# Storing each expert's result with one GpSimd transfer of both halves instead of two

## The reference, cut to what matters

```python
combine = jnp.sum(jax.nn.one_hot(eidx, N_EXPERTS, dtype=jnp.float32) * wk[..., None], axis=1)
y = jnp.zeros((n, dm), jnp.float32)
for e in range(N_EXPERTS):
    h = jax.nn.silu(xn @ w_gate[e]) * (xn @ w_up[e])
    y = y + combine[:, e:e + 1] * (h @ w_down[e]).astype(jnp.float32)
return x + y.reshape(b, l, dm).astype(x.dtype)
```

## Time and profile before

| | |
|---|---|
| median of 3 runs | 1045.94 us (1045.46 to 1047.20) |
| the profiled execution: its time | 1046.94 us |
| its span, first to last instruction | 1045.1 us |
| PE busy | 807.7 us (77%) |
| DVE, ACT, POOL busy | 251.0, 117.8, 148.8 us |
| moved by DMA over the span | 277.47 MB, mean 265 GB/s |
| stores of L493 | 64 of 128 KB |

### The profile page before, as it was taken

One profiled execution on the slowest core, in us unless ns is written; L12 is line 12 of the kernel. 1 busy time (PEld: TensorE's weight loads), 2 busy tenths in 40 slices (PEclk: granted clock), 3 DMA queues, 4 the chain that ended last, 5 costly groups with the idle time before them and its releaser, 6 DMA issues. The chain is left out here.

```text
span 1045.1 us, 9777 instructions
## 1 busy us (share of the span) xinstructions
PE 807.7 (77%) x3738; PEld 469.3 (45%) x3739; DVE 251.0 (24%) x699; ACT 117.8 (11%) x200; POOL 148.8 (14%) x283
## 2 busy tenths in 40 slices
PE   3899999922999899870898787888787787877810
PEld 2688888812988644370333233333233332333300
DVE  4729325754111112224010000000000000000036
ACT  4010121000200011200110010100010100001012
POOL 6300009800023300003010000000000000000040
PEclk9899999965999999955898999999998989889965
DMA  9994114200240170264499999999999999999661
GB/s 345 401 312 162 44 48 128 81 0 1 107 161 1 40 302 1 97 245 174 198 389 428 428 425 430 428 427 428 425 429 428 428 426 428 428 427 426 268 208 68
DMA packets 47643, 277.47 MB, mean 265 GB/s; under 512 B 12186, under 2 KB 13030, under 8 KB 35315
## 3 DMA queue, kind: packets, MB, share of 16 engines
q1 hardware_dynamic: 35388, 238.67, 55.8%
q0 software_dynamic: 11568, 36.58, 9.2%
q10 hardware_dynamic: 646, 1.64, 0.4%
HBM read 243.62 MB, written 33.26 MB: 265 GB/s over the span
## 5 line engine op out<-in xcount | busy, mean ns | idle before, releaser
L1333 PE MATMUL ps<-arena 128*64 128x512 f32 x1024 | 257.9, 661 | 85.7 <-DMA arena<-in_w_exp_up 84.6
L1141 PE MATMUL ps<-arena 128*128 128x272 f32 x1024 | 242.3, 398 | 0.0
L1141 PEld LDWEIGHTS ps<-arena 128*128 128x128 f32 x1024 | 197.2, 193 | 41.2
L1333 PEld LDWEIGHTS ps<-arena 128*64 128x64 f32 x1024 | 89.8, 152 | 231.6 <-issue 229.8
L1071 DVE COPY arena<-ps 128x512 f32<-128x512 f32 x32 | 22.1, 692 | 434.4 <-PE ps L1346 434.4
L1346 PE MATMUL ps<-arena 128*64 128x512 f32 x512 | 116.5, 595 | 1.1 <-DVE arena L1067 1.1
L493 POOL DMA_DIRECT2D y_rows<-arena x64 | 33.2, 523 | 472.4 <-DVE arena L1071 471.5
L1282 PE MATMUL ps<-arena 128*128 128x512 f32 (+1 forms) x160 | 71.1, 605 | 2.9 <-POOL arena L481 2.9
L1346 PEld LDWEIGHTS ps<-arena 128*64 128x64 f32 x512 | 38.1, 137 | 64.2 <-issue 61.2
L699 DVE TENSOR_TENSOR arena<-arena 128x256 f32<-128x256 f32 (+11 forms) x173 | 56.9, 329 | 25.0 <-DMA arena<-in_ssm_b_im 19.2
L651 ACT ACTIVATE arena<-ps 128x512 f32<-128x512 f32 x32 | 19.1, 597 | 330.1 <-PE ps L1333 330.1
(11 more groups left out here) (177 smaller groups left out, 505.1 us busy)
## 6 DMA issues: line engine op xcount, KB each, us to landing
arena<-in_w_exp_gate SPq DMA_DIRECT2D x32, 2048.0 KB, 29.0
arena<-in_w_exp_up SPq DMA_DIRECT2D x32, 2048.0 KB, 19.5
arena<-in_w_exp_down SPq DMA_DIRECT2D x32, 2048.0 KB, 24.6
x_rows<-arena POOLq DMA_DIRECT2D x25, 512.0 KB, 14.3
arena<-in_w_in SPq DMA_DIRECT2D x6, 2048.0 KB, 13.4
arena<-x_rows SPq DMA_DIRECT2D x16, 512.0 KB, 19.4
y_rows<-arena POOLq DMA_DIRECT2D x64, 128.0 KB, 7.1
y_rows<-arena POOLq DMA_DIRECT2D x9, 512.0 KB, 27.2
```

Source lines behind the costliest of these rows:

```text
L1141: last = pe.matmul(dst[:, hh, 0:HALF], w[:, k, m * P:(m + 1) * P], rhs[:, k, hh * HALF:(hh + 1) * HALF], start=(k == 0), stop=(k == kk - 1))
L1333: last = pe.matmul(ps[n * TILE:(n + 1) * TILE, 2 + par, :], x_t[:, k, :], w[:, k, :], start=(k == 0), stop=(k == KD - 1))
```

## The change

L493: the two stores of 64 rows x 512 columns become one of 128 x 512. On the HBM side the 64 x 1024 block is viewed with the half as the outermost dimension (2 x 64 x 512), so that it matches the partitions of `y_sb` in order. The counts waited for are halved with it, at L496 and at L1078. The stores of the overflow path (L503) are left as they were.

```diff
             for e in range(NE):
                 pool.wait_ge(y_ready, e + 1)
-                for half in range(2):
-                    pool.dma_start(y_rows[e * TILE:(e + 1) * TILE, half * F:(half + 1) * F],
-                                   y_sb[e % 2][half * TILE:(half + 1) * TILE]).then_inc(y_stored[e % 2], 16)
+                pool.dma_start(y_rows[e * TILE:(e + 1) * TILE, :].rearrange("t (h n) -> h t n", h=2),
+                               y_sb[e % 2]).then_inc(y_stored[e % 2], 16)
             for par in range(2):
-                pool.wait_ge(y_stored[par], 32 * NP)
+                pool.wait_ge(y_stored[par], 16 * NP)
...
                 if e >= 2:
-                    dve.wait_ge(y_stored[e % 2], 32 * (e // 2))
+                    dve.wait_ge(y_stored[e % 2], 16 * (e // 2))
```

## The result

The changed kernel took 1064.64 us (median of 4, 1061.70 to 1070.19) against 1046.02 (median of 4) for the kernel before on the same chip: a ratio of 1.0178, 95% interval 1.0140 to 1.0215, +18.6 us. The forecast was 1051.5 us, range 1045 to 1060. The direction was right, the size was short by 13 us. The profiled execution took 1061.70 us, with a span of 1059.9.

The account below looks back on a forecast made before the run. The expert loop was taken as bound by the weight stream. 0 (steps 1 to 3) + 1.8 (late weights) + 0 (y_sb wait) + 3.8 (end) = +5.6 us, from the median of 1045.94 to 1051.5 us; range 1045.0 to 1060.0.

Parts of the forecast that it names:

- What bounds the loop: Expert loop: a weight stream at 425 to 430 GB/s; POOL or DVE time costs nothing, later weights are paid in full.
- Step 1: POOL's store issue: one 0.52 us instruction fewer per expert, 31 hidden, the last -0.5 us; bytes and packet number unchanged.
- Step 2: Merged store: outermost dimension 2 puts the whole 128 x 512 store on two DMA engines, 32 packets each.
- step 4: Weights behind the store in the loop: equal engine totals over 8 experts, lateness +1.8 us at the last wait, between 0 and 4.3.
- Step 3: Which two engines on POOL's queue: successive stores move on around the 16, two further each time.
- fixed pair: Rival: the same two engines carry every store, 20.2 us work per expert against 15.9, 1170 us; chance 0.09 including overlapping pairs.
- store chain: Rival: stores landing after over 31.2 us make the L1078 wait the bound, 1075 us or over 1250; chance 0.10.
- Step 5: DVE's wait on y_sb (L1078): a store lands in 26 to 30 us, on average 31.2 allowed; cost 0.
- Step 6: The end, last store to gathers: 32 packets on two engines without weights, +3.8 us including the -0.5 for issue.

Follow-up runs that it names:

- run on ACT's queue: The changed kernel with its single store led by 2 issued by ACT on its own queue (q10) instead of POOL: 1176.70 us, 1.1271.
- 16-engine run: The changed kernel with the HBM side viewed as 128 contiguous pieces, so both sides are led by 128; a probe of time only: 1044.32 us, 0.9985.
- filler run: The kernel before plus, per expert but the last, one tiny GpSimd transfer led by 2 (128 pieces of 16 bytes) into unused scratch: 1059.31 us, 1.0114.
- last-store run: The kernel before, with only the last expert's store made the single transfer led by 2: 1051.62 us, 1.0056.

## Why the prediction was wrong

**What bounds the loop** was right: it is the weight stream, and DVE's new waits are cover. **Step 1** (POOL's issue) was mis-sized and of no weight: the single instruction takes 0.80 us, not 0.52, and 0.23 us of the end's gap were saved instead of 0.5.

**Step 2**, two engines, was right, and read from rows of another queue: 53 GB/s during the last store, and 49 to 52 GB/s in the run on ACT's queue where only two engines had work left. What the Trainium skill states ("DMA: Bandwidth & Descriptors", on why a DMA increments its semaphore by 16) agrees: the largest number up to 16 that divides both leading dimensions. The Trainium skill's rule for kernel authors on the same page, to use one transfer over 128 partitions in place of two over halves, holds in the 16-engine run (1044.32 us) and fails in the changed kernel, which has 128 partitions on one side only.

The step that failed in the main is the last sentence of **step 1**, "The bytes and the packets' number stay the same", taken into **step 4** as "every engine gets the same total over 8 experts". Only the data was counted. GpSimd's queue put packets on the 14 engines without data too (448 per store), by their sizes 64 descriptors on each, as many as the two with data have, and at about 6 ns these cost the weight stream 0.4 us per expert. No row of the kernel before could show it, since all its GpSimd transfers went to 16 engines; but the two loads compared in the earlier trace rows were on SP's queue, and I carried their behaviour over to POOL's queue without a bound for what that queue might add. The bound should have been there: this is the cost of an operation that the trace did not show. It is the missing 11.6 us of the profile, 12.7 in the filler run.

**Step 3**, pairs that move on, is borne out by the rate, since a fixed pair gives 340 GB/s and POOL's queue holds 416, and by the two hand-overs with four packets at once. The rival's price, 1170 us, is near that of ACT's queue, 1176.70; its period was right, and the wait through which it shows was not the one for weights but the one of the store chain. In which order the pairs follow can't be read, since the records do not name the engines.

**Step 4's** +1.8 us of late weights was neither shown nor excluded: with 12.7 and 5.9 known only to a few us, a term of this size can't be told.

**Step 5** was right in its cost, 0, and wrong in its numbers: the store lands after 32.2 us in the loop (median of 24), not 26 to 30; that fillers of other stores take turns ahead of its data would explain it, and was not tested by itself. The wait on `y_sb` was the last one before 28 of 32 copies, which the prediction names as the sign of the store chain, a rival that costs time. It was no such sign: a wait on DVE that is only the last to end costs nothing while PE has other work. From 820 to 940 us the cover wore out in places; PE stood four times for `hidden`, up to 8.8 us, while its waits for weights shrank from 84.6 to 61.6 us in sum. With three buffers these stalls go and the time stays.

**Step 6** was of the right kind, and short by the slow start: landing 9.4 us after issue (8.7 where nothing else was under way) instead of 6.7. The packet records show several of the early packets of such a store at 0.2 to 1.0 us each (up to 1.7 in the last-store run) and then 0.159, as in the stream; why they are slow stays open. So +5.9 for +3.8.

In numbers: 0 + 1.8 + 0 + 3.8 = 5.6 was forecast; 12.7 (filler, not in the sum) + 5.9 (end) = 18.6 was found. The range missed it because its upper end held only the terms that the sum had.

## What to carry to other kernels

Before two transfers are merged, look at the leading dimension of both sides as written in the source: if one is led by a small number, as by 2 here, the merged transfer may run on that few DMA engines. Its 256 KB then took 9 us without the weight stream and 32 us beside it, where on 16 engines each half of 128 KB took 2.4 and 7, and one transfer of 256 KB took 8 beside the stream. A store off the critical path is not free either: on GpSimd's queue it also put descriptors without data of the store on the other engines, and this kernel, bound by its DMA stream, paid for each. Nor is a long wait before an instruction a cost by itself: beside DVE's 433 us of waits on stores PE waited for `hidden` only 29 us, and without those the time was the same. Where PE's own such waits grew to 177 us (ACT's queue), the time grew with them. Packets per queue in two traces of the same bytes (11568 against 25392 here) show this at once.

## What the runs showed of the hardware

- On GpSimd's queue a transfer led by 2 brought 448 packets of 8 bytes beside its 64 of 4 KB; the loss of a saturated stream was about 6 ns per filler descriptor and engine, an estimate, whether they came two (changed kernel, 11.6 us) or 64 to a packet (filler run, 12.7 us). On ACT's queue the same transfer brought none.
- On GpSimd's queue successive transfers led by 2 went to different engines (four packets at once at a hand-over, 416 GB/s beside the weights); on ACT's queue the rate was that of one pair for all of them (340 GB/s).
- Two queues that both had work took turns by packet, whatever the size: 1873 to 1873 in 60 us, with mostly 8 bytes on one side and mostly 16 KB on the other.
